# PEER routing weights: one-hot matmuls against accumulating indirect DMAs, on one core

## What is computed

```
q = (hf @ wq).reshape(T, PEER_HEADS, 2, PEER_HALF)
s = jnp.einsum('thpd,hpkd->thpk', q, keys, ...)
s1, i1 = lax.top_k(s[:, :, 0], 16)            # over 128 keys
s2, i2 = lax.top_k(s[:, :, 1], 16)
top_s, pos = lax.top_k(s1 + s2 over all pairs, 16)
idx = (i1 * 128 + i2) at pos                  # 8 heads x 16 experts a token
w = jax.nn.softmax(top_s, axis=-1)
a = jnp.einsum('td,thkd->thk', hb, u[ib])
out = jnp.einsum('thk,thkd->td', wb * gelu(a), v[ib])
```

## Time and profile before

| | us |
|---|---|
| median of three runs | 4923.87 |
| lowest, highest | 4911.05, 4928.48 |
| the profiled execution | 4906.7 |
| its span | 4905.0 |

### The profile page before, as it was taken

The page is one execution under the profiler, slowest core; times in us unless marked ns, Lnnn a source line. Parts: engine busy times, 40 slices in busy tenths (PEclk is TensorE's granted clock), DMA queues, the critical chain, the costliest instruction groups (busy, mean ns, idle before and its releaser), DMA issues.

```text
span 4905.0 us, 61497 instructions
## 1 busy us (share of the span) xinstructions
PE 4509.8 (92%) x23115; PEld 3849.9 (78%) x23115; DVE 2843.1 (58%) x3097; ACT 1638.3 (33%) x1746; POOL 1395.8 (28%) x643
## 2 busy tenths in 40 slices
PE   7899998999989999699999999999996899999997
PEld 2587777777767877588999988999995778777776
DVE  1234665544436643657799954444444677777776
ACT  0322322333331121324446643444442233322222
POOL 0002332000002300223544556777771011011110
PEclk9899999999989999799999999999998999999998
DMA  8325664000015652453326677777776999989994
GB/s 287 96 78 172 182 184 141 18 28 30 32 39 163 189 170 61 140 167 106 122 102 162 160 235 287 290 286 287 292 283 233 349 342 345 335 315 331 338 341 166
DMA packets 652126, 967.09 MB, mean 197 GB/s; under 512 B 122203, under 2 KB 520595, under 8 KB 599571
## 3 DMA queue, kind: packets, MB, share of 16 engines
q1 hardware_dynamic: 610979, 680.35, 42.0%
q0 software_dynamic: 40928, 285.23, 16.1%
q10 hardware_dynamic: 144, 0.52, 0.0%
HBM read 896.82 MB, written 69.21 MB: 197 GB/s over the span
## 4 chain that ended last, share of the span: by engine, by line
PE 55%; DMA 13%; DVE 11%; issue 10%; ACT 6%; POOL 4%; SPq 1%; ACTq 0%; DVEq 0%; POOLq 0%
PE pp L114 16%; PE pp L116 15%; PE pp L115 15%; DMA gel<-gelu_scratch 10%; POOL pTul L698 3%; DVE vDl L1407 3%; PE pp L2175 3%; ACT vDh L1126 2%; DMA wm<-in_w_mod_dram 1%; PE pp L1806 1%; DVE mred L1287 1%; DVE gel L1692 1%; PE pp L1964 1%; DVE acc L1686 1%; PE pp L2236 1%
## 5 line engine op out<-in xcount | busy, mean ns | idle before, releaser
L698 POOL TENSOR_TENSOR pTul<-pT,pTuh 128x1024 fp32r<-128x1024 f32 x256 | 731.5, 2857 | 522.9 <-ACT pTuh L1056 507.2
L114 PE MATMUL pp<-h2h,pTuh 128*128 128x384 f32 x2048 | 732.9, 358 | 18.9 <-POOL pTul L698 17.4
L114 PE MATMUL pp<-vDh,coh 128*128 128x512 f32 x1536 | 614.6, 400 | 108.1 <-DVE col L1407 107.8
L116 PE MATMUL pp<-h2h,pTul 128*128 128x384 f32 x2048 | 691.7, 338 | 0.0
L115 PE MATMUL pp<-h2l,pTuh 128*128 128x384 f32 x2048 | 690.1, 337 | 0.0
L1673 DVE SCALAR_TENSOR_TENSOR ring<-ring,h2tok 128x2048 f32<-128x2048 f32 x128 | 357.6, 2796 | 480.7 <-DMA ring<-in_peer_u_dram,sidx 480.0
L115 PE MATMUL pp<-vDl,coh 128*128 128x512 f32 x1536 | 609.1, 397 | 0.0
L116 PE MATMUL pp<-vDh,col 128*128 128x512 f32 x1536 | 608.5, 396 | 0.0
L674 POOL TENSOR_TENSOR mbuf<-mbuf,silu 128x2048 f32<-128x2048 f32 x64 | 260.5, 4070 | 995.8 <-DMA mbuf<-in_w_mod_dram 995.1
L114 PEld LDWEIGHTS pp<-vDh,coh 128*128 128x128 f32 x1536 | 295.7, 193 | 187.0 <-DVE vDl L1407 73.5
L712 POOL DMA_INDIRECT ring<-in_peer_v_dram,sidx x128 | 151.7, 1186 | 938.2 <-DVE acc L1686 917.2
(11 more groups left out here) (343 smaller groups left out, 8959.7 us busy)
## 6 DMA issues: line engine op xcount, KB each, us to landing
pu<-in_peer_u_dram SPq DMA_DIRECT2D x128, 1024.0 KB, 6.8
vraw<-in_peer_v_dram SPq DMA_DIRECT2D x128, 1024.0 KB, 8.1
mbuf<-in_w_mod_dram SPq DMA_DIRECT2D x64, 1024.0 KB, 5.7
wraw<-in_w_in_dram SPq DMA_DIRECT2D x48, 1024.0 KB, 8.5
wt<-route_scratch SPq DMA_DIRECT2D x128, 384.0 KB, 7.2
gel<-gelu_scratch SPq DMA_DIRECT2D x128, 384.0 KB, 9.1
wm<-in_w_mod_dram SPq DMA_DIRECT2D x16, 2048.0 KB, 8.5
gelu_scratch<-act_g SPq DMA_DIRECT2D x128, 192.0 KB, 1.9
```

The lines of the kernel that those rows point to most:

```text
L114: pe.matmul(out, lh, rh, start=first, stop=False)
L116: return pe.matmul(out, ll, rh, start=False, stop=last)
L698: pool.tensor_tensor(pTul[:, c, :], pT[:, c, :], pTuh[:, c, :].bitcast(fp32), ALU.subtract).then_inc(u_lo, 1)
```

## The change

- The one-hot stage goes: no transposes of the picks, one-hots, routing matmuls, copies or stores.
- VectorE turns each pick into a cell number of the DRAM table, expert x 384 + token (`ridx`), with the weight beside it (`rw`). GpSimd adds the weights into the table by **accumulating indirect DMAs**: one for each of the 128 slots of each of three token blocks, 384 in all, of 128 single words. Since two heads of a token may pick the same expert, the first scatter of a head waits until all earlier ones of its token block have landed. The table, 25 MB, is zeroed before, in eight pieces by SyncE in the attention loop.
- Of the scatters, 42 stand in up blocks 14 to 27, three behind each block's low parts; the other 342 stand three behind each gather.
- From up block 28 (`TOPS`) on u takes another way: ScalarE rounds it straight from PSUM (`late_hi`), VectorE subtracts straight from PSUM (`u_rest`), `pT` isn't used, `pTuh` and `pTul` are doubled, and GpSimd has no low parts any more.
- The gathers begin at that point, in a ring of three buffers. VectorE runs four dots, then in each block: rest, dot, rest, dot. From block 95 on, 66 of the 128 axpys take the dots' places. In the down part the other 62 are spread, and stand ahead of the product.
- In the down part ScalarE rounds v before the coefficients.

```diff
+TOPS = 28
+SCATTER_AT = 14
+EXP_AT = (5, 11, 17, 23)
+COEF_AT = 94
+            def zero_route(p):
+                sp.dma_start(route_flat[:, bass.ds(p * ZROW, ZROW)].rearrange("j (a n) -> j a n", n=512),
+                             zeros[:, :].unsqueeze(1).to_broadcast([P, ZROW // 512, 512])).then_inc(z_stored, 16)
...
             with sp.Fori(1, HEADS // 2) as p:
                 sp.wait_ge(pw_lo, 2 * p)
                 pair_loads(p)
+                zero_route(p)
...
-            with pool.Fori(0, LATE + 2) as i:
-                u_low(i, 0)
-                u_low(i, 1)
-            pool.wait_ge(tk_chosen, 2)
-            for ss in r_stored:
-                pool.wait_ge(ss, 64 * (TD // RT // 2) + 16)
-            k = 0
-            for i in range(LATE + 2, NK):
-                for h in range(2):
-                    u_low(i, h)
-                    if k < SLOTS and (2 * i + h) % 6 != 5:
-                        gather_u(k)
-                        k += 1
...
+            def gather(k):
+                if k >= 3:
+                    pool.wait_ge(ring_used, k - 2)
+                pool.indirect_dma_start(ring[k % 3][:, :], None, u_rows if k < SLOTS else v_rows,
+                                        bass.IndirectOffsetOnAxis(ap=sidx[:, k % SLOTS:k % SLOTS + 1], axis=0)
+                                        ).then_inc(ring_in[k % 3], 16)
+
+            def scatter(n):
+                b, k = n // SLOTS, n % SLOTS
+                if k == 0:
+                    pool.wait_ge(tk_chosen, b + 3)
+                elif k % TOPK == 0:
+                    pool.wait_ge(r_stored[b], 16 * k)
+                pool.indirect_dma_start(route_cells, bass.IndirectOffsetOnAxis(ap=ridx[b][:, k:k + 1], axis=0),
+                                        rw[b][:, k:k + 1], None, compute_op=ALU.add).then_inc(r_stored[b], 16)
...
+            for i in range(SCATTER_AT, TOPS):
+                first_lows(i)
+                for _ in range(3):
+                    scatter(n)
+                    n += 1
+            pool.wait_ge(tk_chosen, 2)
+            pool.wait_ge(tk_chain, SCORE_READ)
+            for k in range(2 * SLOTS):
+                gather(k)
+                for _ in range(3):
+                    if n < DB * SLOTS:
+                        scatter(n)
+                        n += 1
...
+            def late_hi(i, s, h):
+                act.wait_ge(u_turned, 2 * i + h + 1)
...
+                act.activation(pTuh[s][:, 8 * h:8 * h + 8, :], pp[h][:, :].rearrange("p (c j) -> p c j", c=8),
+                               ACT.Copy).then_inc(u_hi, 1)
...
+            def u_rest(i, h):
+                s = i % 2
+                c = slice(8 * h, 8 * h + 8)
+                dve.wait_ge(u_hi, 2 * i + h + 1)
+                lo(pTul[s][:, c, :], pp[h][:, :].rearrange("p (c j) -> p c j", c=8), pTuh[s][:, c, :]).then_inc(u_sub, 1)
...
+            while k < 4:
+                dot(k)
+                k += 1
+            for i in range(TOPS, NK):
+                if i == COEF_AT + 1:
+                    dve.wait_ge(scoef_set, 1)
+                    ch.link(dve.tensor_tensor(scoef[:, :], scoef[:, :], sw[:, :], ALU.mult))
+                for h in range(2):
+                    u_rest(i, h)
+                    if k < SLOTS:
+                        dot(k)
+                        k += 1
+                    elif i > COEF_AT:
+                        axpy(k - SLOTS)
+                        k += 1
+            in_up = k - SLOTS
...
             for n in range(2, NK):
-                down_coef(n)
                 for k in range(ax_before(n), ax_before(n + 1)):
                     axpy(k)
+                down_coef(n)
                 down_v_lo(n)
```

357 lines of the change are left out of this document (134 added, 223 removed).

## The result

The changed kernel takes 5121.07 us (median of 4 runs, 5113.27 to 5125.09) where the kernel before takes 4926.17 us (median of 4, 4911.05 to 4935.42): ratio 1.0399, 95% interval 1.0382 to 1.0417. It is slower, inside the range and on the side that had the larger chance (0.48), but the step is 195 us where the forecast was 28. The profiled execution took 5125.09 us (span 5123.3), 218 us more than the profiled one of before.

What follows compares the result with a forecast made beforehand. TensorE was taken to bound the kernel before, GpSimd to pace the changed up blocks: 118 us lost there less 90 gained in the down part, +28 on 4906.7, 4935 us, or 4952 on the runs' scale; range 4780 to 5150.

Steps and rivals of the forecast that it cites:

- part 3: Up blocks from 28: GpSimd paces TensorE through VectorE's in-order rests and dots, 7.0 us a gather, 118 us lost.
- the first term of the cycle: GpSimd's issue of three scatters and one gather, all at a gather's price of 1.24 us: 4.96 us a gather.
- The dot's toll: Up blocks from 28: each VectorE dot holds back GpSimd's indirect DMAs, costing 1.5 us a gather.
- Head ends: Up blocks from 28: 19 scatters wait for 16 predecessors to land, 3.1 us each, 0.5 us a gather.
- VectorE's own time: Up blocks from 28: rest about 1.2 us plus dot 2.4, 3.6 of 5.1 us, so VectorE isn't the bound.
- Part 1: Up part: routing matmuls and one-hots go, up to 138 us to be had; zeroing the table costs nothing.
- Part 2: Up blocks 14 to 27: three scatters after each second low part cost about 12 us, bounds 0 and 25.
- Part 4: Down part: 13 us from an earlier start and 77 from pairs at TensorE's 8.16 us, 90 us gained.
- (d): Rival: accumulating scatters hold their transfer queue 1.9 us each; cycle 8.9 us, time 5167 us; chance 0.15.
- (a): Rival: GpSimd keeps up in the up blocks, a scatter costing 0.8 us or less; 4736 us; chance 0.15.
- (b): Rival: GpSimd bound but cheap, indirect DMAs following each other at a 0.15 us gap; cycle 6.2, 4862 us; chance 0.20.
- (c): Rival: scatters land on their own 1.9 us after issue, head ends cost 1 us; cycle 6.65, 4912 us; chance 0.12.

## Why the prediction was right and wrong

- **The bound** (part 3): right in kind. GpSimd paces the up blocks from 28 to 83, by VectorE's in-order chain, and not after. The pitch was 16.66 and not 14. Of the 190 us between forecast and span, 146 lie in this one cycle.
- **The step that failed** is the first term of the cycle, "four indirect DMAs x 1.24 = 4.96 us", with its ground, "No scatter stands in the trace; the nearest rows are the gathers ... and I take their price". Measured: three scatters at 1.55 + 0.30 and a gather at 0.97 + 0.30, 6.82 us. The term was 1.9 us too small. With writing scatters, which do have a gather's price, the cycle came out at 6.92 where 7.0 was forecast, so the rest of the cycle held.
- **The dot's toll**: 1.5 forecast, 1.03 measured in the changed kernel, 1.39 and 1.44 where the scatters are shorter or fewer. Mis-sized, by -0.5 us a cycle: the blocked instruction began 1.06 us into the dot and not 0.6.
- **Head ends**: 0.5 us a cycle forecast, 46.7 us over 113 cycles measured, 0.41; 14 of some length and 3.3 us each instead of 19 and 3.1. Right.
- The sum 7.0 + 1.9 - 0.5 - 0.1 is the 8.3 measured; the toll, too high by chance, hid a quarter of the scatters' surcharge.
- **VectorE's own time** (1.2 us a rest): 1.22, right, and it is not stopped by GpSimd.
- **Part 1**: 138 us available; the kernel without the scatters at the gathers has 1358.4 us from first to last GELU, 63 more than the 1295 of 127 blocks at 10.2: 30 in the top stage, 21 in the block with the four dots, 18 at block 114, less 6 for a block of 10.14. The zeroing cost next to nothing, right. The step of 18 us more at block 114, where u's load stands behind those of v, weights and GELU rows in SyncE's queue and TensorE waits 15.6 us for it in the changed kernel, I did not have. The kernel before has such a step too, between windows of the earlier trace rows (TensorE waits 12.2 us for u there):

```profile
L1061 ACT ACTIVATE act_g<-pp x2: 491/492/492, 2941.7 to 2966.6; 128x384 f32<-128x384 f32 x2
PE pp L2175 <- DMA pu<-in_peer_u_dram: 12.2, 1, 12.2
```

- **Part 2**: 21 us instead of 12, within its bounds of 0 and 25, and not from the scatter's price. With writing scatters, at the 3.7 us for three that the prediction took, the same 25 steps are 280.3 us against 282.5 in the changed kernel and 261.3 before:

```profile
L1064 ACT ACTIVATE act_g<-pp x26: 491/492/494, 2270.2 to 2550.5; 128x384 f32<-128x384 f32 x26
```

  So 2 us of the 21 go with the price; what the other 19 come from, and why less was absorbed than forecast, stays open.
- **Part 4**: 93.5 us instead of 90. 14 us at the start (13), 120 x 0.63 = 76 (77), 4 at the end. Right in size, with some luck, since the kernel before's second profile would make the steady part's gain 92 us (9.05 against 8.28 a pair). Which of the three edits is the reason isn't shown.
- **Rivals**: (d), "the accumulate is slow", was nearest in number (cycle 8.9, 5167 us) and right in that the adding costs. But I put the price into the transfer queue, at 1.9 us a scatter, where it is on GpSimd itself; by luck 1.85 us is almost the same. (a) would have needed 0.8 us. (b) fell by the gap of 0.30 between neighbours. (c) fell with the waits of 3.3 us.

What misled was one price: the result turned at a cycle of 6.75 us, three of the four DMAs in a cycle were of a kind that no row shows, and the cases should have been laid out along the price of one scatter, on both sides of the gather's.

## What to carry to other kernels

An indirect DMA that adds is not an indirect DMA that copies: take the price of each form from its own row, and where there is none, say at which price the forecast turns. Before work goes to an engine with idle time, add up what it then does per step of the bound engine; under that step's time it is free (one scatter a gather), over it every microsecond counts (two and three), and a version that spread the same work over more steps, with some edits beside, turned 4% slower into 3.8% faster. An in-order engine between two others (VectorE here) carries the slower one's pace to the faster.
